# Gate projection of the last stage: eight block products per pair of tiles become seven

## The reference, cut to what matters

```python
h = h + concatenate([attention, pooling]) @ w_out
hn = rmsnorm(h, g_ffn_norm)
h = h + (silu(hn @ w_gate) * (hn @ w_up)) @ w_down
gate = sigmoid(rmsnorm(h, g_ple_norm) @ w_ple_gate)   # 1024 x 1024
h = h + gate * (p @ w_ple_proj)                       # 256 x 1024
```

## Time and profile before

| | before |
|---|---|
| median of 3 runs | 2041.3 us (2040.14 to 2041.78) |
| profiled execution, span | 2043.8 us |
| PE busy | 2014.7 us (99%) |
| DVE busy | 1365.8 us (67%) |
| ACT busy | 900.5 us (44%) |
| POOL busy | 409.9 us (20%) |
| DMA, mean | 143 GB/s |

### The profile page before, as it was taken

How to read it: one execution, slowest core, us unless ns; L and a number is a source line. 1 busy time by engine, 2 the same in 40 slices (tenths; PEclk the granted TensorE clock), 3 DMA queues, 4 the chain that set the end, 5 groups by cost and what they waited for, 6 DMA issues and landing times.

```text
span 2043.8 us, 26178 instructions
## 1 busy us (share of the span) xinstructions
PE 2014.7 (99%) x9565; PEld 1667.4 (82%) x9565; DVE 1365.8 (67%) x1904; ACT 900.5 (44%) x1461; POOL 409.9 (20%) x534
## 2 busy tenths in 40 slices
PE   8999999999999999999999999999999999999998
PEld 7887877877788888888888888888888888888887
DVE  4686664767686665665888765966566566987763
ACT  4585743757433333333333553533333333334542
POOL 5554644645420000000000220000000000001220
PEclk9999999999999999999999999999999999999999
DMA  8667556563933223224815029432322328342143
GB/s 194 196 186 249 192 187 219 176 237 128 347 133 122 89 70 96 83 73 165 313 57 170 21 78 237 139 119 68 95 87 69 99 80 290 138 148 81 50 134 103
DMA packets 195488, 292.10 MB, mean 143 GB/s; under 512 B 14661, under 2 KB 116429, under 8 KB 194080
## 3 DMA queue, kind: packets, MB, share of 16 engines
q1 hardware_dynamic: 172672, 212.97, 34.3%
q0 software_dynamic: 22544, 77.46, 11.2%
q10 hardware_dynamic: 144, 0.00, 0.0%
HBM read 223.25 MB, written 67.51 MB: 142 GB/s over the span
## 4 chain that ended last, share of the span: by engine, by line
PE 86%; DVE 5%; DMA 3%; issue 2%; ACT 2%; POOL 1%; SPq 0%; ACTq 0%; DVEq 0%; POOLq 0%
PE bank L2646 13%; PE bank L2648 13%; PE bank L2650 13%; PE bank L2685 7%; PE bank L2683 7%; PE bank L2684 7%; PE bank L2345 5%; PE bank L2347 5%; PE bank L2346 5%; PE bank L2321 2%; PE bank L2323 2%; PE bank L2322 2%; PE bank L2414 1%; DMA w_parts<-w_split 1%; PE bank L2427 1%
## 5 line engine op out<-in xcount | busy, mean ns | idle before, releaser
L2646 PE MATMUL bank<-a_hi,ring_hi 128*128 128x512 f32 x1232 | 480.4, 390 | 1.1 <-DVE ring_lo L1940 0.7
L2650 PE MATMUL bank<-a_hi,ring_lo 128*128 128x512 f32 x1232 | 479.9, 390 | 0.0
L2648 PE MATMUL bank<-a_lo,ring_hi 128*128 128x512 f32 x1232 | 479.9, 390 | 0.0
L2646 PEld LDWEIGHTS bank<-a_hi,ring_hi 128*128 128x128 f32 x1232 | 231.3, 188 | 50.1 <-DVE ring_lo L1940 1.4
L2650 PEld LDWEIGHTS bank<-a_hi,ring_lo 128*128 128x128 f32 x1232 | 231.3, 188 | 48.1
L2648 PEld LDWEIGHTS bank<-a_lo,ring_hi 128*128 128x128 f32 x1232 | 231.4, 188 | 47.5
L2683 PE MATMUL bank<-d_hi 128*128 128x512 f32 x616 | 240.1, 390 | 0.0
L2684 PE MATMUL bank<-d_lo,d_hi 128*128 128x512 f32 x616 | 240.0, 390 | 0.0
L2685 PE MATMUL bank<-d_hi,d_lo 128*128 128x512 f32 x616 | 239.9, 389 | 0.0
L1419 ACT ACTIVATE d_hi<-keep 128x1024 fp32r<-128x1024 f32 x132 | 139.8, 1061 | 201.9 <-PE bank L2685 184.9
L999 POOL DMA_DIRECT2D hidden_T<-hid x88 | 47.6, 541 | 770.5 <-DVE hid L1976 751.2
(11 more groups left out here) (271 smaller groups left out, 3889.9 us busy)
## 6 DMA issues: line engine op xcount, KB each, us to landing
w_parts<-w_split POOLq DMA_DIRECT2D x88, 512.0 KB, 4.6
hidden_T<-hid POOLq DMA_DIRECT2D x88, 256.0 KB, 2.3
raws<-in_w_gate SPq DMA_DIRECT2D x80, 256.0 KB, 4.7
raws<-in_w_up SPq DMA_DIRECT2D x80, 256.0 KB, 5.2
keep<-hidden_T SPq DMA_DIRECT2D x66, 256.0 KB, 3.8
raw<-in_w_ple_gate SPq DMA_DIRECT2D x64, 256.0 KB, 4.2
keep<-in_w_down SPq DMA_DIRECT2D x44, 256.0 KB, 4.1
other<-hidden_T SPq DMA_DIRECT2D x44, 256.0 KB, 6.8
```

Source lines behind the costliest of these rows:

```text
L2646: mm(dst[:, :], wh[:, g, cols], a_hi[o][:, k, :], start=fresh and k == 0, stop=False, skip_group_check=True)
L2648: mm(dst[:, :], wh[:, g, cols], a_lo[o][:, k, :], start=False, stop=False, skip_group_check=True)
L2650: ins = mm(dst[:, :], wl[:, g, cols], a_hi[o][:, k, :], start=False, stop=k == 3, skip_group_check=True)
```

## The change

For a pair of tiles the 1024 x 1024 gate matrix and the rows of the two tiles are cut in 2 x 2 blocks of 512, and seven products of 48 matmuls, `G_ONE` to `G_FOUR`, take the place of eight. The sums on the weight side do not depend on the tiles. They are made once, with their high and low parts, and kept in DRAM (`g_split`: 14 panels of high and low part, 1 MB each). This is done in blocks c = 2 to 9 of `ffn_section(0)`, in four rounds of two blocks. A round loads four blocks of 128 x 512, POOL makes four sums, and seven items follow, three in the first block of the round (after beats 2, 3, 4) and four in the second (after beats 1 to 4). An item is a high part on ACT into the single buffer `gw_hi`, a low part on POOL, and two stores of 256 KB from POOL's queue. ACT may write the next high part only when all stores of the items before have landed (`gate_stored`).

In the late stage SP loads the 14 panels back in three slots, once for each pair. DVE makes the sums of the rows, ACT and DVE split them. Single products are copied out of PSUM by ACT, second products added by DVE (`add_products`), tanh is taken in SBUF for three of four blocks, and the final addition to the rows moves from DVE to POOL for these (`add_gated`). The factor 0.5 moves into the copy of `proj`. PE's order is now: both projections of the first tile, products one and two, both projections of the second tile, products six, five, seven, three and four, with 24 matmuls for each panel or projection. The order of `a_part_hi` in half 1 is new and partly moved behind the handover.

```diff
-A_ORDER = (0, 1, 3, 4, 2, 5, 6)
+A_ORDER = ((0, 1, 3, 4, 2, 5, 6), (0, 2, 1, 3, 4, 5, 6))
+A_LOW_ORDER = ((0, 1, 2, 3, 4, 5, 6), (0, 2, 1, 3, 4, 5, 6))
...
+    g_split = nc.dram_tensor("gate_split", (G_PANELS, 2, P, PANEL), F32, kind="Internal")
...
+        g_parts = [sb(f"g_parts{i}", [P, 2, PANEL], at, F32R) for i, at in enumerate((96, 80, RING0))]
...
+            def load_gate(half, n):
+
+                slot, _ = gate_slot(half, n)
+                if n == 0:
+                    sp.wait_ge(d_lo_done, STEPS_D * half + FPAIRS * FOURTH)
+                    sp.wait_ge(sumt4, FPAIRS * (half + 1))
+                    if half == 0:
+                        sp.wait_ge(*gate_stored(4 * PRODUCTS))
+                elif n == 1:
+                    sp.wait_ge(d_lo_done, STEPS_D * (half + 1))
+                elif n == 2:
+                    sp.wait_ge(lo_done, split_of(ple_at(half) + 1) + 1)
+                else:
+                    sp.wait_ge(*gate_panels_done(half, (n - 3) // 2, (n - 3) % 2))
+                for part in range(2):
+                    sp.dma_start(g_parts[slot][:, part, :].bitcast(F32), g_split[n, part]).then_inc(x_landed[slot], 16)
 
...
+                load_gate(half, 0)
+                load_p(gb)
+                for n in range(1, G_PANELS):
+                    if half == 0:
+                        for which in {7: (2,), 8: (3, 1), 9: (0,)}.get(n, ()):
+                            load_a(1, which)
+                    if half == 0 and n == 13:
+                        load_pair(1, 0, (0, 1))
+                    load_gate(half, n)
+                if half == 0:
+                    load_pair(1, 0, (3, 2))
...
+            def add_gated(half, n):
+                tile, e = G_BLOCKS[n // 4 % 4]
+                pool.wait_ge(ple_mul, n + 1)
+                v = h2[tile][:, 4 * e + n % 4, :]
+                nc.gpsimd.tensor_tensor(v, gate_buffer(n), v, ALU.add).then_inc(ple_out, 1)
+
+            def gate_blocks(k):
+                if k == 0:
+                    pool.wait_ge(ring_lo_done, 2 * OPS)
+                    pool.wait_ge(n2_done, 4 * NT)
+                else:
+                    pool.wait_ge(*gate_stored(PRODUCTS * k))
...
+            def gate_block_sums(k):
+                pool.wait_ge(consts, CONSTS + 64 * (k + 1))
+                b11, b12, b21, b22 = gw[0], gw[1], gw[2], gw[3]
+                nc.gpsimd.tensor_tensor(gw[4][:, :], b12[:, :], b11[:, :], ALU.subtract).then_inc(wp_lo_done, 1)
+                pool.wait_ge(wp_lo_done, 1 + (PRODUCTS + 4) * k + 1)
+                nc.gpsimd.tensor_tensor(gw[5][:, :], b22[:, :], gw[4][:, :], ALU.subtract).then_inc(wp_lo_done, 1)
+                nc.gpsimd.tensor_tensor(b12[:, :], b22[:, :], b12[:, :], ALU.subtract).then_inc(wp_lo_done, 1)
+                pool.wait_ge(wp_lo_done, 1 + (PRODUCTS + 4) * k + 2)
+                nc.gpsimd.tensor_tensor(gw[6][:, :], b21[:, :], gw[5][:, :], ALU.subtract).then_inc(wp_lo_done, 1)
+
+            def gate_block_low(k, i):
+                at = gate_block_of(i)
+                pool.wait_ge(wp_hi_done, 1 + PRODUCTS * k + i + 1)
+                nc.gpsimd.tensor_tensor(gw_lo[at][:, :], gw[at][:, :], gw_hi[:, :].bitcast(F32),
+                                        ALU.subtract).then_inc(wp_lo_done, 1)
+                n, cols = 2 * i + k // 2, slice(k % 2 * T, (k % 2 + 1) * T)
+                pool.dma_start(g_split[n, 0][:, cols], gw_hi[:, :].bitcast(F32)).then_inc(band_stored, 16)
+                pool.wait_ge(wp_lo_done, 1 + (PRODUCTS + 4) * k + 4 + i + 1)
+                pool.dma_start(g_split[n, 1][:, cols], gw_lo[at][:, :].bitcast(F32)).then_inc(band_stored, 16)
+
+            def gate_weights(c, o):
+                k, second = divmod(c - G_PREP_FROM, 2)
+                if not 0 <= k < 4:
+                    return
+                if o == 0 and not second:
+                    gate_blocks(k)
+                if o == 1 and not second:
+                    gate_block_sums(k)
+                if o in G_ITEM_AT[second]:
+                    gate_block_low(k, G_ITEM_AT[second].index(o) + 3 * second)
 
...
+                    for o in range(OPS):
+                        if o == 0 and c:
+                            store_hid(half, c - 1, 3)
+                        if half == 0 and o < 2:
+                            gate_weights(c, o)
+                        if o in (2, 5, 6):
+                            store_hid(half, c, (2, 5, 6).index(o))
+                        if half == 0 and o >= 2:
+                            gate_weights(c, o)
...
+                for b in range(16):
+                    n = 16 * half + b
+                    if b < 12:
+                        add_gated(half, n)
+                    if half == 0 or b < 12:
+                        store_out(half, n)
...
+                if half:
+                    if o == 0:
+                        act.wait_ge(pp, 16)
+                    elif o in (1, 3, 4):
+                        act.wait_ge(ple_out, {1: 12, 3: 8, 4: 12}[o])
+                    elif o == 5:
+                        act.wait_ge(*gate_panels_done(0, G_FOUR, 1))
+                    elif o == 6:
+                        act.wait_ge(*gate_panels_done(0, G_FOUR, 0))
...
+            def gate_block_hi(k, i):
+                at = gate_block_of(i)
+                done = PRODUCTS * k + i
+                act.wait_ge(consts, CONSTS + 64 * (k + 1))
+                if i >= 2:
+                    act.wait_ge(wp_lo_done, 1 + (PRODUCTS + 4) * k + 4)
+                if done:
+                    act.wait_ge(*gate_stored(done))
+                nc.scalar.activation(gw_hi[:, :], gw[at][:, :], ACT.Copy).then_inc(wp_hi_done, 1)
+
+            def gate_weights(c, o):
+                k, second = divmod(c - G_PREP_FROM, 2)
+                if 0 <= k < 4 and o in G_ITEM_AT[second]:
+                    gate_block_hi(k, G_ITEM_AT[second].index(o) + 3 * second)
 
...
+                for b in range(NB):
+                    copy_gate(half, G_FIVE, b)
+                operand_hi(half, G_FOUR, 0)
+                operand_hi(half, G_FOUR, 1)
+                for b in range(4, 8):
+                    gate_tanh(half, b)
+                if half == 0:
+                    a_part_hi(1, 1)
+                for b in range(8, 12):
+                    gate_tanh(half, b)
+                if half == 0:
+                    ring_part_hi(1, 0)
+                    a_part_hi(1, 2)
+                for b in range(12, 16):
+                    gate_tanh(half, b)
...
+            def gated_rows(half, b):
+
+                n = 16 * half + b
+                tile, e = G_BLOCKS[b // 4]
+                dve.wait_ge(pp_copied, copied_count(half, (tile, e), b % 4))
+                for piece, cols in enumerate(drained(n)):
+                    dve.wait_ge(sig, n + piece + 1)
+                    buf = gate_buffer(n)[:, cols]
+                    nc.vector.scalar_tensor_tensor(out=buf, in0=buf, scalar=1.0, in1=proj[tile, e][:, b % 4, cols],
+                                                   op0=ALU.add, op1=ALU.mult).then_inc(ple_mul, 1)
+                    if b < 12:
+                        continue
+                    dve.wait_ge(ple_mul, n + piece + 1)
+                    dve.wait_ge(ple_out, 16 * half + 12)
+                    v = h2[tile][:, 4 * e + b % 4, cols]
+                    nc.vector.tensor_tensor(v, buf, v, ALU.add).then_inc(ple_out, 1)
+
...
+                for i in (G_FIVE, G_SEVEN, G_THREE):
+                    for r in range(2):
+                        operand_lo(half, i, r)
...
+                for first in (4, 8):
+                    add_products(half, first)
+                    for b in range(first + 1, first + 4):
+                        add_products(half, b)
+                        gated_rows(half, b - 1)
+                    gated_rows(half, first + 3)
+                    if half == 0 and first == 4:
+                        a_rest(1, 2)
+                if half == 0:
+                    ring_part_lo(1, 0)
+                    a_rest(1, 1)
+                for b in range(12, 16):
+                    gated_rows(half, b)
 
...
+            def gate_product(half, i, r):
+                n = 2 * i + r
+                slot, landed_there = gate_slot(half, n)
+                pe.wait_ge(x_landed[slot], landed_there)
+                pe.wait_ge(nlo, operand_count(half, i, r))
+                hi, lo = gate_operand(i)
+                fresh = i in (G_ONE, G_TWO, G_FIVE)
+                for b in range(NB):
+                    if r == 0:
+                        if i == G_ONE:
+                            pe.wait_ge(pp_copied, copied_count(half, (0, 1), b))
...
+                        elif i == G_SEVEN:
+                            pe.wait_ge(pp_copied, copied_count(half, G_SIX, b))
+                        elif i == G_THREE:
+                            pe.wait_ge(pp_copied, copied_count(half, G_FIVE, b))
+                        else:
```

(93 more changed lines are left out.)

548 lines of the change are left out of this document (273 added, 275 removed).

## The result

The change made the kernel slower. Median of nine runs 2047.5 us (2040.9 to 2050.2) against 2041.3, ratio 1.0025 with a 95% interval of 1.0016 to 1.0034; forecast was 2033.0 (2023 to 2044). Nine runs of the kernel before lie between 2040.0 and 2045.1. The profiled execution has a span of 2047.0 us, 3.2 over that of before.

What follows compares the result with a forecast made beforehand. TensorE, busy 99% of the span, was taken as the bound. Terms -21.7 + 4.8 + 0.4 + 1.0 + 4.6 + 0.5 + 2.1 = -8.3 took the span from 2043.8 to 2035.5, the median to 2033.0 us (range 2023 to 2044).

Steps and rivals of the forecast that it cites:

- Matmuls, -21.7: Late stages of both halves: 96 matmuls removed at 0.2264 us each, -21.7 us.
- Weight preparation, +4.8: ffn_section(0): u3 copies on ACT delayed behind store waits, 1.2 us in each of four rounds, +4.8.
- the 0.6 of the forecast's own round numbers: First block of a round: u3 copy ends at 703.0 against 702.4 needed, 0.6 us late.
- The rival on landings of 3.0: Stores in ffn_section(0) blocks land after 3.0 us or later, not 2.3: +8.4, time 2041.4, no change; chance 0.15.
- +11 in the forecast's own term: Upper case for weight preparation in ffn_section(0): +11 us if the landing of stores is 3.0.
- A landing of 3 or more: Sign against the forecast: stores into g_split landing after 3 us or more.
- Late stage, +0.4 and +1.0: Late stage: second projection's bank wait +0.2 per half, +0.4 (0 to 2); DMA transfers +1.0 (0 to 5).
- The bank wait forecast: Late stage: gaps eat some of the 0.7 us slack before the second projection needs its bank, +0.2 per half.
- Handover and clock, +4.6 + 0.5 + 2.1: Start of half 1: ring_lo stall of 5.3, 0.7 there before, +4.6; operand copy +0.5; half-speed clock afterwards +2.1.
- The reason given for POOL's pace, 1.33 + 0.54 + gaps: Handover: each of POOL's eight late additions takes 1.33, plus 0.54 store issue and 0.2 of gaps.
- The slower rival (transfers set the pace): Late stage: 16.7 MB move at 240 GB/s, 69.6 us instead of 54; time 2047.6; chance 0.10.
- a fall only behind waits of 5 us: Second product of half 1: one wait of about 5 us, with the granted clock at 0.50 behind it.

Runs made afterwards that it cites:

- the fastest version: Changed kernel with items 1 and 2 behind the u3 copies, handover and copy reorderings, high part stored alone, late additions on DVE: 2021.7 us, ratio 0.9904 to the kernel before.
- the run on the whole handover: Changed kernel with items 1 and 2 behind the u3 copies, POOL's additions before stores, tanh and rows before the operand, ring 1 parts earlier: 2028.2 us, ratio 0.994.
- the items behind u3: Changed kernel with items 1 and 2 of each round's first block moved from beats 3 and 4 to behind beats 5 and 6: 2030.0 us, ratio 0.9939.

## Why the prediction was wrong, step by step

- **Matmuls, -21.7: right.** The late stages became 18.7 shorter, and 2.2 more are PE's waits for projection copies; with the two longer ones gone they were 100.2 and 99.9, so 20.8 of the saving came through, and the fastest version shows nearly the same (20.7).
- **Weight preparation, +4.8: the step that failed. It was +17.1.** The order of the chain was right, its durations were not. In the first round item 1 started 18.7 behind the hidden store in place of 17.7, because the four loads landed 3.9 us after their last issue (3.5 to 4.6 over the four rounds), not 2.5. Item 2 followed item 1 by 5.8 in place of 4.8, because the second store of item 1 landed 3.2 after its issue, not 2.3. I had taken the landing from lone hidden stores, while here two stores follow each other on a queue: the first of a pair landed 2.3 after its issue in the median, the second 3.3 (2.3 to 7.3), both together 3.0. The sums of 7.1 were as taken (7.0).
  These two steps of 1.0 stand on top of the 0.6 of the forecast's own round numbers: PE was 2.6 late, where I took 1.2. PE's lateness shows as two waits, since group 0's copy of u3 stands behind item 1 and `ring_hi`, but it is set by group 1's copy alone. The idle time of the rows is 10.9 in all. They understate each wait by 0.16 (a matmul is shown for 0.39 while the next begins 0.23 behind it), and the first matmul behind a wait takes 0.1 more (0.30 to 0.38 to the next start): 2.3 for nine.
  And the forecast had no clock term there. Two falls of 1.7 make 3.4. Together 16.6, and 0.6 stay when all waits are gone: 17.2 against 17.1. The rival on landings of 3.0 had this mechanism, and at 4.8 + 8.4 = 13.2 nearly its size without the clock (10.9 + 2.3 = 13.2); that it agrees to the tenth is luck, since it shared out the delays otherwise. The same case stands as +11 in the forecast's own term. A landing of 3 or more was named as a sign that the forecast is wrong, and it came.
- **Late stage, +0.4 and +1.0: it was +3.0, by other causes.** Transfers cost 0.2 at most: `g_parts` landed 4.6 us from issue in the median. The bank wait forecast was 0.2 per half, as it came. The 0.9 per half was not foreseen: ACT's projection copies stand behind squares that wait for POOL's additions, and these took 1.9 each beside DVE.
- **Handover and clock, +4.6 + 0.5 + 2.1 = +7.2: measured +7.2, the sum partly by luck.** The wait is 6.2 against the forecast 5.3, so +5.5; the operand's copy cost nothing, since PE had no wait behind the one for `ring_lo`; the clock cost 1.9. The reason given for POOL's pace, 1.33 + 0.54 + gaps, was wrong although six of seven additions started 2.2 to 2.3 behind the one before, near the 2.07 of the forecast: taking the issues out shortened the wait by 0.2 us. It is POOL and DVE taking turns. The rule of the Trainium skill ("SBUF — State Buffer", section "Who interferes with whom"), that a DVE instruction with two SBUF inputs and a GpSimd one that reads SBUF exclude each other, I had applied to the sums only; it was the one to apply here too. The runs agree with it (3.90 for two additions beside DVE's products, and 0.69 for each DVE product with POOL out of the way).
- **The slower rival (transfers set the pace)** did not occur. Its 2047.6 meets the measured 2047.5 by luck: slower came through a mechanism that I had priced too low.

What stays open: how much of the small gain from earlier loads is due to the later hidden value and how much to the landings was not separated, and what decides whether the clock falls behind a short wait is not known.

## What to carry to other kernels

Work put "beside" a full engine was not free here, because an in-order queue held copies that this engine needs behind waits for a DMA. List every instruction behind such a wait, not the last one only, and let a buffer's release wait for its own store alone: moving two copies behind the needed ones, or not waiting for the second store, gave back 16 us of a change that had looked like a loss. Take a landing time from transfers issued as the new ones will be.

## What the runs showed of the hardware that was not expected

- Short waits of PE can cost the clock. Of the last waits of twelve rounds (three profiled executions) six, 1.57 to 1.78 us long, were followed by no lower clock, six, 1.81 to 1.89, by a fall to 0.50, whatever the wait before it was (none to 1.57). But length alone does not decide: in the run on the whole handover the clock stayed at 1.00 behind a wait of 2.85 that ended at 1297.29, with one of 1.20 some 8 us before.

```profile
1298.00:1300.00 2.00, 2.00 (x10) 1.65 (x10) 2.00 (x2) 2.00 (x2) 0.00 (x0) 1.00 1.22 294
```

  The forecast had looked for a fall only behind waits of 5 us. The falls may be a part of the spread of the changed kernel's runs, 9.3 us, against 3.3 with the items behind u3; but the kernel before spread over 5.1 and one later version over 6.8, so this is not shown.
- POOL and DVE with two inputs each in SBUF take turns: additions start 1.92 apart, and an addition beside DVE's work is counted as 1.29 alone or as up to 2.5 in a pair (4.99 for two).
